# Four modulation units of a two-block transformer kernel put at other places of the weight stream

## The reference

```
mod = silu(c) @ w_ada + b_ada                    # 6 x 2048 values from a 2048 x 12288 matrix
sh1, sc1, gt1, sh2, sc2, gt2 = split(mod, 6)
h = rms_norm(x, g_pre_mix) * (1 + sc1) + sh1
proj = h @ w_in                                  # GLU, q, k, v, index q / k / w, gates
mixed = (g_conv * conv_branch(...) + g_attn * sparse_attn_branch(...)) @ w_o
x = x + gt1 * rms_norm(mixed, g_post_mix)
h = rms_norm(x, g_pre_ffn) * (1 + sc2) + sh2
x = x + gt2 * rms_norm((silu(h @ w_gate) * (h @ w_up)) @ w_down, g_post_ffn)
```

## Time and profile before

| | |
|---|---|
| runs | 2616.86, 2621.10, 2621.43 us, median 2621.1 |
| profiled execution | 2622.12 us, its span 2620.3 us |
| TensorE busy | 2566.8 us, 98% of the span |
| VectorE busy | 1688.4 us, 64% |
| ScalarE busy | 1279.2 us, 49% |
| moved from memory | 578 MB, mean 221 GB/s |
| mean granted TensorE clock | 0.993 of full speed |

### The profile page before, as it was taken

The page is one execution under the profiler, slowest core; times in us unless marked ns, Lnnn a source line. Parts: engine busy times, 40 slices in busy tenths (PEclk is TensorE's granted clock), DMA queues, the critical chain, the costliest instruction groups (busy, mean ns, idle before and its releaser), DMA issues.

```text
span 2620.3 us, 28988 instructions
## 1 busy us (share of the span) xinstructions
PE 2566.8 (98%) x11654; PEld 2104.2 (80%) x11654; DVE 1688.4 (64%) x1937; ACT 1279.2 (49%) x1775; POOL 3.9 (0%) x11
## 2 busy tenths in 40 slices
PE   7999999999989999999999999999999999999998
PEld 5788778878878888888888788888788888888886
DVE  7999899989875555555555645666545454445455
ACT  4445677754454444444444555554544444444443
POOL 0000000000000000000000000000000000000000
PEclk9999999999999999999999999999999999999999
DMA  9998456877956566666554554445455555555553
GB/s 374 355 346 312 162 206 216 293 282 285 376 174 224 209 220 233 242 226 220 207 208 178 176 180 174 162 175 193 162 192 192 193 203 190 196 187 188 192 193 129
DMA packets 80569, 578.14 MB, mean 221 GB/s; under 512 B 8990, under 2 KB 9254, under 8 KB 10673
## 3 DMA queue, kind: packets, MB, share of 16 engines
q1 hardware_dynamic: 78768, 566.92, 59.8%
q10 hardware_dynamic: 1154, 6.67, 0.6%
q0 software_dynamic: 512, 2.69, 0.3%
HBM read 574.13 MB, written 3.68 MB: 221 GB/s over the span
## 4 chain that ended last, share of the span: by engine, by line
PE 84%; DVE 7%; DMA 3%; ACT 3%; issue 1%; DVEq 0%; ACTq 0%; SPq 0%
PE bank L689 80%; DVE wlo L1530 2%; DMA raw<-in_w_in 2%; DMA raw<-in_w_o 1%; PE bank L641 1%; ACT whi L1014 1%; DVE raw L1540 1%; DVE X L1525 1%; PE bank L801 0%; ACT SS L1190 0%; PE bank L784 0%; PE bank L727 0%; PE bank L935 0%; DVE SC L1687 0%; PE bank L849 0%
## 5 line engine op out<-in xcount | busy, mean ns | idle before, releaser
L1530 DVE TENSOR_TENSOR wlo<-raw,whi 128x1024 fp32r<-128x1024 f32 x882 | 1074.3, 1224 | 879.9 <-ACT whi L1014 877.1
L1014 ACT ACTIVATE whi<-raw 128x1024 fp32r<-128x1024 f32 x882 | 931.5, 1059 | 1246.0 <-PE bank L689 1105.3
L689 PE MATMUL bank<-whi,HTh 128*128 128x512 f32 x2560 | 704.7, 397 | 9.7 <-ACT HTh L1014 6.1
L689 PE MATMUL bank<-wlo,HTh 128*128 128x512 f32 x2560 | 687.3, 390 | 5.7 <-DVE wlo L1530 5.6
L689 PE MATMUL bank<-whi,HTl 128*128 128x512 f32 x2560 | 689.3, 391 | 0.1
L689 PEld LDWEIGHTS bank<-wlo,HTh 128*128 128x128 f32 x2560 | 480.9, 188 | 109.3 <-DVE wlo L1530 8.4
L689 PEld LDWEIGHTS bank<-whi,HTl 128*128 128x128 f32 x2560 | 482.7, 189 | 104.2 <-DVE HTl L1525 1.0
L689 PEld LDWEIGHTS bank<-whi,HTh 128*128 128x128 f32 x2560 | 472.2, 189 | 108.9 <-issue 11.1
L1540 DVE CUSTOM_DVE_ANT_0 raw<-raw,GT,VECS 128x2048 f32<-128x2048 f32 x96 | 225.0, 2347 | 0.6 <-DMA raw<-in_w_ada 0.6
L689 PE MATMUL bank<-whi,ACTh 128*128 128x512 f32 x704 | 190.6, 392 | 0.0
L689 PE MATMUL bank<-whi,ACTl 128*128 128x512 f32 x704 | 189.0, 389 | 0.0
(11 more groups left out here) (227 smaller groups left out, 1200.1 us busy)
## 6 DMA issues: line engine op xcount, KB each, us to landing
raw<-in_w_in SPq DMA_DIRECT2D x128, 1024.0 KB, 4.9
raw<-in_w_ada SPq DMA_DIRECT2D x96, 1024.0 KB, 6.4
raw<-in_w_gate SPq DMA_DIRECT2D x88, 1024.0 KB, 4.8
raw<-in_w_up SPq DMA_DIRECT2D x88, 1024.0 KB, 4.8
raw<-in_w_down SPq DMA_DIRECT2D x88, 1024.0 KB, 4.8
raw<-in_w_o SPq DMA_DIRECT2D x16, 1024.0 KB, 7.1
raw<-in_w_out SPq DMA_DIRECT2D x16, 1024.0 KB, 4.8
raw<-in_w_attn_out SPq DMA_DIRECT2D x8, 1024.0 KB, 4.9
```

What stands on the lines that cost most here:

```text
L689: i = e.matmul(bank[2 * ch.st + t][:, :], (xl if ps == 1 else xh)[:, k, tk(t)], (lo if ps == 2 else hi)[:, j * 512:j * 512 + 512], start=c ...
L1014: return e.activation(dst, src, ACT.Copy, scale=scale)
L1530: e.tensor_tensor(lo, src, r32(hi), S_).then_inc(lo_done, 1)
```

## The change

In `k1` and `v1` a share of 0.5 is given, so that modulation units are put in there. In w_o the share stays 0.9 for the first three chunks and is 0 for the last. The four scale steps begin at slots 200, 204, 208 and 212 (w_o's start is 194) in place of all at 222.

```diff
-    p.cols(p.chunk("k1", 0, "h", "ACT"), "w_in", 7, range(4), 4)
-    p.cols(p.chunk("v1", 0, "h", "ACT"), "w_in", 9, range(4), 4)
+    p.cols(p.chunk("k1", 0, "h", "ACT"), "w_in", 7, range(4), 4, 0.5)
+    p.cols(p.chunk("v1", 0, "h", "ACT"), "w_in", 9, range(4), 4, 0.5)
...
-        p.cols(p.chunk("wo", j, "mix", "DVE", apart=j == 3), "w_o", j, range(4), 4, 0.9)
+        p.cols(p.chunk("wo", j, "mix", "DVE", apart=j == 3), "w_o", j, range(4), 4, 0.9 if j < 3 else 0.0)
...
         for j in R(4):
-            lane.begin(M["wo"] + 28, mod_job(4, j))
+            lane.begin(M["wo"] + 6 + 4 * j, mod_job(4, j))
```

## The result

The changed kernel takes 2624.57 us (median of 20 runs, 2622.69 to 2627.13), the kernel before 2619.58 in the 20 runs beside it (2616.86 to 2625.06): ratio 1.002, 95% interval 1.0014 to 1.0026. It is 5.0 us slower (3.7 to 6.8 by the interval). The forecast was +5.0, or 2626.1; it started from the 2621.1 of three runs, and in these 20 the kernel before is 1.5 faster, by which the time lies under it.

What follows compares the result with a forecast made beforehand. TensorE, busy nearly throughout, was taken to bound the kernel. Terms 6.35 + 0.8 - 2.1 gave +5.0 us, 2627.1 from the profiled 2622.1, and 2626.1 us for the median, 1.0 lower; range 2619.0 to 2630.5.

Steps and rivals of the forecast that it cites:

- What bounds: Whole kernel: TensorE is busy nearly the whole span, so time changes only where it stands still or runs at half clock.
- term 1: Keys and values: four units delay VectorE's low halves, making TensorE's piece 98 6.35 us late; +6.35, bounds 2.3 and 9.1.
- The wait for `wlo` in the keys: Sign in the profile after: TensorE's wait for low halves there grows from 4.1 to about 10 us.
- Term 2: Keys and values: longer TensorE idles lower the granted clock, losing between 1.8 and 3.4 us after piece 98; +0.8 taken.
- The rival that the clock falls more than once: Keys and values: further unhidden clock falls cost 1.8 or 3.6 us, net +7 to +9, 2629; chance 0.15.
- Term 3: End of w_o: TensorE's waits of 0.74 and 1.39 us at pieces 224 and 225 go; -2.1, bounds 0 and -5.5.
- Term 4: Rest: moved scale steps and earlier FFN units cost 0; uncovered, the steps would cost 0.6 us and a unit 2.27.
- VectorE's lead: Rival, keys and values: idle lead swallows the units, terms 1 and 2 are 0, leaving -2.1, 2619.0 us; chance 0.12.
- The clock did not stay up at w_o's end: Rival, w_o's end: clock fall goes or halves, 1.7 to 3.4 us more won, net about +2.5, 2623.5; chance 0.15.
- Late loads: Rival, k1 and v1: loads come late, costing a part of 7.1 us more, 2631 us; chance 0.03.

Runs made afterwards that it cites:

- e1: Changed kernel with its four units in keys and values summed over only 64 of 2048 columns; 2617.71 us against 2618.98 for the kernel before (ratio 0.9992).
- e6: Changed kernel with a second, unused 2048-wide VectorE product after each of the same four units; 2633.98 us, ratio 1.0053 to the kernel before.
- e9: Kernel before with only GpSimd's 1.5 MB write moved into the FFN; 2619.54 us against 2619.86 (ratio 0.9996).
- e12: Kernel before with one modulation unit moved from ahead of w_o's piece 224 to ahead of piece 86; 2616.41 us against 2619.97 (ratio 0.9989).
- e5: Kernel before with two units put ahead of pieces 86 and 90 and w_o's last two gone; 2618.44 us against 2619.86 (ratio 0.9994).
- e11: Kernel before with one unit moved from ahead of w_o's piece 224 to ahead of piece 98; 2621.20 us against 2619.25 (ratio 1.0006).
- e2: Changed kernel with w_o's third chunk free of modulation units in place of its last; 2624.41 us against 2618.98 for the kernel before (ratio 1.0016).
- e3: Changed kernel with the four scale steps back at slot 222; 2624.32 us, ratio 1.0019 to the kernel before.
- e8: Changed kernel with w_o's first chunk free of modulation units in place of its last; 2624.16 us against 2619.86 for the kernel before (ratio 1.0015).
- e7: e4 with GpSimd's 1.5 MB write also put off until 16 pieces into the FFN; 2618.09 us against 2619.86 for the kernel before (ratio 0.9994).
- e10: e7 with four units moved from the attention's output to the convolution's output; 2615.08 us against 2619.25 for the kernel before (ratio 0.9983).
- e4: Changed kernel with its four units ahead of pieces 80, 82, 84 and 86; 2617.35 us against 2618.98 for the kernel before (ratio 0.9993).

## Why the prediction was right

**What bounds, and term 1.** Right by its steps. The delay carried forward was to be 4.08 at piece 95 and 6.35 at piece 98. Measured from the w_kiwi mark (1.33 earlier after), piece 98's low half starts at 332.25 + 1.33 = 333.58 against 327.46, 6.12 later; piece 95's 314.85 + 1.33 = 316.18 against 312.33, 3.85. Both are 0.2 under the forecast. TensorE's new wait ahead of piece 95 was to be 1.9 and is 1.68. e1 and e6 show the cause from both sides (less work on VectorE takes the loss away, more adds to it one for one). The other kernels repeat the sum. "Delay" is how much later piece 98's low half starts than in the kernel before, both counted from w_kiwi; "clock" is what the keys lose beyond it:

| kernel | units ahead of | delay carried forward | delay measured | clock |
|---|---|---|---|---|
| e9 | none | 0 | 0.00 | 0.25 |
| e12 | 86 | 0 | 0.00 | 0.26 |
| e1 | four thin ones (0.21 each) | 0.4 | 0.38 | 0.79 |
| e5 | 86, 90 | 1.81 | 1.57 | 0.09 |
| e11 | 98 | 2.27 | 2.26 | 0.79 |
| after, e2, e3, e8 | 86, 90, 94, 98 | 6.35 | 6.12 to 6.14 | 0.73 to 0.79 |

The wait for `wlo` in the keys was to be about 10 us and is 8.7. What is missing is the wait ahead of piece 97, which the first fall of the clock covers.

**Term 2, the clock.** The size came out in this pair of profiles, and that is in part luck: the keys lost 6.91, of which 6.12 is the delay of piece 98, so 0.8 is left for the clock, the value taken. In the rows, after the idle of 4.61 the matmuls run at half clock from the first, after the 2.40 of before only towards the end of the group (1.29). e11 gives the same with one unit. But the length of the idle does not decide it alone: after 2.59 in e1 the matmuls are slow from the first too, and after 2.41 in e7 and 2.40 in e10 the clock does not fall at all. From the group behind the last wait to the second group behind the first attention product it is 3.23 us in e7 and e10, 4.71 to 4.79 in six kernels with idles of 2.34 to 2.59 (before and e9 among them), and 5.56, 5.74, 4.79 and 5.17 in after, e2, e3 and e8. So a fall there cost the kernel before 1.5 us, and the changed order 1.6 to 2.5: between 0 and 1.0 more. What decides it after an idle of 2.4 no run separates. The rival that the clock falls more than once happened in part: there were two falls, but the first was hidden, as the prediction says of a fall among these pieces. The Trainium skill ("TensorE: Matmul & The Clock Gate", "HAM oscillation — how this bites in real kernels") has the cost paid at every long wait. The trace agrees in part: a slow stretch of its own came after the waits ahead of pieces 96 (2.41) and 98 (4.61), none after the 1.68 ahead of 95, and only that of piece 98, behind which TensorE sets the pace, cost time.

**Term 3, the end of w_o.** Right in sign, and in size as far as the profiles tell: -2.1 expected, -2.88 measured in one profile of each, and -1.4 to -3.6 over the eight kernels with 10 units in w_o. Behind each stall TensorE also loses a little in the next groups: from piece 224's first matmul to the last group the two profiles close up by 4.72 - 2.70 = 2.0 us (start times 723.32 and 728.04, 730.32 and 733.02), where the second wait alone was counted with 1.39. The reason given for the step was wrong in one point. I wrote that the waits go because there are no units from piece 218 on. e2 and e8 have three units there and no waits, and e11 and e12 have all but the last and no waits at pieces 224 and 225 either. It is not the last chunk that counts. What the runs bear out is lateness that builds up along the stage: 14 units gave 92.04 and 92.03 us (before and e9), 13 gave 90.23 and 89.74, 12 gave 90.43, and 10 gave 88.46 to 90.59 (eight kernels, e10 left out). How the lateness grows, in the ring of buffers or on VectorE, was not separated. The profiles name a third candidate, the memory traffic itself: in the kernel before the DMA engines are busy 0.89 to 1.02 in every window of 10 us from 648 to 728 (335 to 424 GB/s), in the changed one 0.79 and 0.52 in the last two windows ahead of 731. But in e12 they are 0.87 to 1.02 busy from 655 to 725, and TensorE waits for nothing at the end, so this is not shown either. The remaining waits for `whi` in the middle of w_o, none to 1.6 us, differ between profiles of the same order of loads (after 0.34, e3 1.04), so single profiles don't tell 10 units from 12 or 13.

**Term 4.** Right: e3 for the steps; for the FFN's earlier units there is no wait on TensorE in the rows, and the rest of the kernel is 0.4 shorter, if anything.

**The sum.** The mechanism was right in the keys; at w_o's end the sign and size were right and a part of the reason was wrong. That the +5.0 agrees to the tenth is luck. The stages of the two profiles add up to +3.6, the interval of the times is 3.7 to 6.8, and the clock's term alone could have been 0 to 1.0.

**The rivals.** VectorE's lead did not swallow four units, but it does swallow one (e12). The clock did not stay up at w_o's end: 0.95 and 0.88 in the windows from 720 and 740 give 1.0 + 2.4 = 3.4 us, as before. Late loads played no part in the keys of the changed kernel (e1, and the rows of VectorE), though they seem to as soon as units stand closer and earlier (e4, one profile).

## What to carry to other kernels

Before moving work into an engine's queue, carry its delay forward along that queue: idle by idle, up to the first instruction that another engine already waits for. The price grows with each unit: the first cost no delay at piece 98, two cost 1.57, and the fourth its full length, with some clock on top. And take away only as much as a late place needs: one unit out of w_o, put ahead of piece 86, gave 3.6 us (0.5 to 5.2), four units put ahead of pieces 86 to 98 gave 5.0 the other way. And before a stage of one profile is trusted to a microsecond, look at a second profile of the same stage: here the keys agreed to 0.3, w_o only to 2.

## What was not expected of the hardware

Loads of 1 MB that land in 4.8 to 8.4 us in e7 took 7.2 to 11.6 in e4, where GpSimd's 1.5 MB write ran beside the same eight loads from 255 to 285 (one profile of each). In the kernel before, with the write and four loads there, they took 5.2 to 7.2.

After the same three idles of TensorE (0.52, about 1.25, 2.4 us) the granted clock fell in the kernel before, e4, e9 and e12, and stayed at 1.00 in e7 and e10.
